# Start addresses of the large SBUF tiles in a two-block transformer kernel: from residue 128 to residue 0 modulo 2048 bytes

## The chip, the cores and the metric

The kernel runs on one NeuronCore of a Trainium2 chip. The metric is the device time of one execution in microseconds; the median of three runs before is 3795.62 us (3795.41 to 3798.67).

## The reference

The input is x, [1, 512, 1024] in float32: 512 tokens (T), width 1024 (D). Two blocks are computed.

- First block: an adaptive norm from a condition vector, one projection to eight times the width, a gated recurrence in eight heads, a gated depthwise convolution of 31 taps with a layer norm, a merge and an output projection; then an expert layer in which each token picks 16 of 16384 experts in each of eight heads. The kernel computes the expert layer as two dense products with a matrix of gates between them.
- Second block: a dilated-window attention with a squared-ReLU MLP of width 4096, then a differential attention with such an MLP, with norms ahead of each, and a last norm.

In outline:

```python
h = x + g1 * (merge(recurrence(u @ w_in), conv(u @ w_in)) @ w_out)
h = h + g2 * ((gelu(u2 @ U.T) * gates) @ V)          # 16384 experts, dense
for mix in (dilated_attention, differential_attention):
    h = h + mix(norm(h) @ w_qkv) @ w_o
    h = h + relu(norm(h) @ w_in) ** 2 @ w_out
```

All of it is in float32; nearly all of the arithmetic is in matrix products with 512 tokens as the moving side.

## The kernel before, in words

**Layout.** Activations stand transposed: partition p of tile [P, KT, T] holds feature 128 k + p of all 512 tokens. KT is 8, so such a tile has 8 slices of 512 float32 (2048 bytes) in each partition. The residual stays in `hT`.

**Panels.** Every large product is cut into panels: 128 output features by 1024 input features, 8 slices of 128x128 weights. There are 568 panels, kept in one list in the order of use (`panels`); the queue of SyncE loads them one after the other into a ring of four buffers (`ring`, `load`, L318 to L321). The first 16 are used by VectorE; the other 552 are *split* panels for TensorE.

**The split.** To keep the accuracy of float32 with one-pass float32r matmuls, a weight panel and its moving tile are each held as a high and a low part. ScalarE copies `ring` to `high_w` (rounded, L819 and L1096), GpSimd writes ring - high_w back into `ring_r` (L2014). `uT_r`, `ring_r` and `sq_r` are float32r names for the same bytes as `uT`, `ring` and `sq`. TensorE does three matmuls for each slice k (`panel`, L364 to L383), 24 for a panel, each with 512 moving columns and weights of its own:

```python
t_.matmul(out, wh, xh, start=(k == 0), stop=False)            # L377
t_.matmul(out, wh, xl, start=False, stop=False)               # L378
last = t_.matmul(out, wl, xh, start=False, stop=(k == KT-1))  # L379
```

wh is a slice of `high_w`, wl one of `ring_r`, and (xh, xl) is the moving pair. `two_panels` (L394 to L396) does the same for two panels at once. The pairs are:

| Panels | Count | xh, xl |
|---|---|---|
| heads and gates of the first block | 64 | uT_r, ulo (which is part_x) |
| w_a | 8 | sq_r, og_r (part0) |
| w_b | 8 | cvh (part_x), cv_r (part1) |
| w_out | 8 | uT_r, sga_r (part2) |
| peer_wq, expert up, qkv (twice), MLP up (twice) | 256 | uT_r, sq_r |
| expert down | 128 | part0, part1 or part2, part3 in turn |
| output projection of the attentions | 16 | kT_r (part1), qT_r (part0) |
| MLP down (twice) | 64 | part0, part1 or part2, part3 in turn |

So 208 panels stream both parts from `part0` to `part3`, 24 stream one of the two from there, and 320 neither.

**Order.** The order of the work is written out by hand for each engine in a function of its own; semaphores `w_slot`, `hi_ready`, `lo_ready`, `gemm_done` and `bank_free` hand a panel from SyncE's queue to ScalarE, GpSimd and TensorE and its result from PSUM to VectorE or ScalarE. VectorE makes the low and high parts of the hidden tiles (L1391, L1392) and adds each output panel to `hT` (L1716, L1719).

**Places in SBUF.** Tiles are placed one after the other, in the order in which they are declared, each at the next multiple of 32 bytes; the first of this program begins at byte 16,512 of each partition (8 x 2048 + 128). `arena` is 27520 float32, on which most other tiles are views; `part0` to `part3`, `between` and `part_x` are float32r names for stretches of it. This gives:

| Tile | First byte before | modulo 2048 |
|---|---|---|
| hT | 16512 | 128 |
| uT, uT_r | 32896 | 128 |
| ring, ring_r | 49280 | 128 |
| high_w | 65664 | 128 |
| sq, sq_r | 82048 | 128 |
| st | 98432 | 128 |
| cc, cst, ones, act_out | 106624, 108320, 109344, 109856 | 128, 1824, 800, 1312 |
| arena, part0 | 112640 | 0 |
| part1, part2, part3 | 129024, 145408, 161792 | 0 |
| part_x | 192640 | 128 |

A slice of weights takes 512 bytes in each partition, so slice k of a weight buffer begins at 128 + 512 k modulo 2048; a slice of a moving tile takes 2048 bytes.

Of the kernel before, what the change touches and what calls it, by code (L numbers as in the profile page):

```python
# [27 lines left out]
P = 128  # L28
T = 512
D = 1024  # L30
KT = D // P
# [33 lines left out]
NCOLS = _n  # L65
# [52 lines left out]
def build(nc, panels, xT, cols, consts, lmask, keysT, oh, rel, blam, ada_rest, outT, gdram, adram, btab, strips_dram):  # L118
    F32 = mybir.dt.float32
# [5 lines left out]
    with ctx:  # L125
        def sb(name, shape, dt=F32):
            return ctx.enter_context(nc.sbuf_tensor(name, shape, dt))

        F32R = mybir.dt.float32r
# [8 lines left out]
            return ctx.enter_context(nc.semaphore(name))  # L138

        ps = ctx.enter_context(nc.psum_tensor("ps", [P, 8, 512], F32))  # L140
        hT = sb("hT", [P, KT, T])
        BF16 = mybir.dt.bfloat16
        uT, uT_r = both("uT", [P, KT, T])
# [2 lines left out]
        sq, sq_r = both("sq", [P, KT, T])  # L146
        st = sb("st", [P, 4, T])
        ms, sr, rt, rstd = (st[:, n, :] for n in range(4))
        cc = sb("cc", [P, NCOLS])
        cst = sb("cst", [P, 2 * P])  # L150
        ones = sb("ones", [P, P])
        act_out = sb("act_out", [P, 1, T])
        rbs = sb("rbs", [35, 16])
        ada = sb("ada", [P, 48])
        small = sb("small", [P, 96])
        sb("to_128_bytes", [P, 24])
        with nc.sbuf_tensor("arena", [P, 27520], F32) as arena:
            pass

        parts = [sb(f"part{n}", [P, KT, T], F32R) for n in range(4)]  # L160
        between_r = sb("between", [P, 20000 - 4 * KT * T], F32R)
        part_x = sb("part_x", [P, KT, T], F32R)
        sb("rest", [P, 27520 - 20000 - KT * T])
        ident, iota = cst[:, 0:P], cst[:, P:2 * P]

        def view(at, *shape):
# [2056 lines left out]
```

How the kernel before makes its waits and increments, by code:

```python
    def wait(self):  # L90
        self.eng.wait_ge(self.sem, self.value())
# [6 lines left out]
    def wait_but_last(self):  # L99
        v = self.count - 1
        for reg, per in self.regs:
            v = reg * per + v
        self.eng.wait_ge(self.sem, v)
# [209 lines left out]
        @block.sync  # L314
# [3 lines left out]
            def load(i, j):  # L318
                sp.wait_ge(gemm_done, i * RING + (j + 1))
                sp.dma_start(ring[:, j], panels[i * RING + (RING + j)]).then_inc(w_slot[j], 16)
# [3 lines left out]
                sp.dma_start(gi[:, g, k, :].rearrange("p (a t) -> p a t", a=TT),  # L325
                             gdram[:, 8 * g + k:8 * g + k + 1].rearrange("a i j t -> j (i a) t")).then_inc(g_in[g], 16)
            at_gates = (8 * Q_PEER + 4 * PER_TILE * TT + 8) // RING
            with sp.Fori(0, at_gates) as i:
                for j in range(RING):
                    load(i, j)
            for j in range(RING):
                load(at_gates, j)
                if j == 0:
                    sp.wait_ge(g_out, 272)
                for k in range(4):
                    first_gates(j // 2, 4 * (j % 2) + k)
            with sp.Fori(0, 8 * Q_END // RING - 2 - at_gates) as i:
                for j in range(RING):
                    load(i + (at_gates + 1), j)
            for n in range(4):
                sp.wait_ge(u_ready, 50 + 2 * n)
                sp.dma_start(outT[:, 2 * n:2 * n + 2], sq[:, 2 * n:2 * n + 2]).then_inc(out_done, 16)
            sp.wait_ge(out_done, 64)
```

## Time and profile before

| | |
|---|---|
| Median of three runs | 3795.62 us |
| Span of the profiled execution | 3793.6 us |
| TensorE busy | 3674.0 us (97%), 16460 matmul records |
| VectorE busy | 2314.3 us (61%) |
| GpSimd busy | 1476.4 us (39%) |
| ScalarE busy | 1316.0 us (35%) |
| DMA | 486.59 MB, mean 128 GB/s |

The profile gives no time for its own execution beyond the span; the median of the runs is 2.0 us above that span, which is what lies around it. A matmul's duration in these rows (some 390 ns) overlaps with its neighbours', so what a matmul costs in a dense stretch is the distance from its start to the start of the next, its *pace*; a count of matmuls in a window holds the one or two that were already running when the window began.

### The profile page before, as it was taken

The page shows a single profiled execution, that of the slowest core. Times are in us where ns is not written, and L with a number is a line of the kernel's source. Part 1 is how long each engine was busy: PE and PEld are TensorE (multiplying, and loading weights), DVE is VectorE, ACT ScalarE, POOL GpSimd, SP SyncE. Part 2 cuts the span into 40 slices and gives each one's busy share as a digit, 9 for nine tenths or more (in the row PEclk, how much of TensorE's full clock was granted, in tenths as well). Part 3 has the DMA queues.
Part 4 walks back from the last instruction along what each step waited for, and adds up shares of the span by engine and source line. Part 5 has one row for each costly group of instructions (what it writes and reads, how often), then busy time and mean ns, then how long its engine had stood idle before and what let it go on. Part 6 is the DMA issues. An engine that isn't in the chain of part 4 may idle for free.

```text
span 3793.6 us, 48518 instructions
## 1 busy us (share of the span) xinstructions
PE 3674.0 (97%) x16460; PEld 2908.2 (77%) x16460; DVE 2314.3 (61%) x3639; ACT 1316.0 (35%) x1805; POOL 1476.4 (39%) x684
## 2 busy tenths in 40 slices
PE   6999999999999999999999999989999999999998
PEld 4787777788888888878888887855788877358886
DVE  5787996155757585188888775346564431658541
ACT  4554323334343434321111113246322232663221
POOL 2322443333333333344444443454344444124442
PEclk8999999999999999999999999989999999999999
DMA  5435322233546463865555652221222222112222
GB/s 203 150 109 189 113 89 79 90 98 120 188 146 193 137 214 116 261 215 186 186 185 184 197 174 90 95 68 44 67 95 99 96 89 99 59 46 92 95 98 79
DMA packets 267076, 486.59 MB, mean 128 GB/s; under 512 B 16770, under 2 KB 148226, under 8 KB 266658
## 3 DMA queue, kind: packets, MB, share of 16 engines
q1 hardware_dynamic: 90816, 304.12, 24.3%
q10 hardware_dynamic: 176132, 180.76, 14.6%
q8 instruction: 82, 1.34, 0.1%
q14 instruction: 46, 0.37, 0.0%
HBM read 415.48 MB, written 84.02 MB: 132 GB/s over the span
## 4 chain that ended last, share of the span: by engine, by line
PE 87%; DVE 5%; issue 4%; ACT 3%; DMA 1%; DVEq 0%; POOL 0%; SPq 0%; ACTq 0%; POOLq 0%
PE ps L377 25%; PE ps L378 25%; PE ps L379 25%; PE ps L617 3%; PE ps L716 2%; DVE ps L1665 1%; DMA ring<-panels 1%; PE ps L489 1%; PE ps L693 1%; PE ps L425 1%; PE ps L706 1%; PE ps L698 1%; ACT arena L1240 0%; PE ps L596 0%; ACT arena L1246 0%
## 5 line engine op out<-in xcount | busy, mean ns | idle before, releaser
L2014 POOL TENSOR_TENSOR ring_r<-ring,high_w 128x1024 fp32r<-128x1024 f32 x552 | 1361.0, 2467 | 2086.4 <-ACT high_w L819 1623.5
L377 PE MATMUL ps<-uT_r,high_w 128*128 128x512 f32 x2608 | 1037.9, 398 | 4.3 <-DVE part_x L1402 2.0
L379 PE MATMUL ps<-uT_r,ring_r 128*128 128x512 f32 x2608 | 1017.8, 390 | 0.0
L819 ACT ACTIVATE high_w<-ring 128x1024 fp32r<-128x1024 f32 x440 | 464.3, 1058 | 1272.2 <-PE ps L379 1112.4
L378 PE MATMUL ps<-sq_r,high_w 128*128 128x512 f32 x2032 | 791.2, 389 | 0.0
L378 PE MATMUL ps<-part,high_w 128*128 128x512 f32 x1840 | 728.5, 396 | 0.0
L377 PE MATMUL ps<-part,high_w 128*128 128x512 f32 x1664 | 670.3, 403 | 11.4 <-issue 4.9
L379 PE MATMUL ps<-part,ring_r 128*128 128x512 f32 x1664 | 658.8, 396 | 0.0
L377 PEld LDWEIGHTS ps<-uT_r,high_w 128*128 128x128 f32 x2608 | 491.7, 189 | 111.0 <-issue 12.0
L379 PEld LDWEIGHTS ps<-uT_r,ring_r 128*128 128x128 f32 x2608 | 490.8, 188 | 103.4
L1391 DVE SCALAR_TENSOR_TENSOR part<-arena 128x512 fp32r<-128x512 f32 x192 | 463.8, 2416 | 6.6
L378 PEld LDWEIGHTS ps<-sq_r,high_w 128*128 128x128 f32 x2032 | 381.8, 188 | 78.3 <-issue 1.9
L378 PEld LDWEIGHTS ps<-part,high_w 128*128 128x128 f32 x1840 | 348.1, 189 | 88.2 <-issue 8.2
L377 PEld LDWEIGHTS ps<-part,high_w 128*128 128x128 f32 x1664 | 314.5, 189 | 94.0 <-issue 13.7
L379 PEld LDWEIGHTS ps<-part,ring_r 128*128 128x128 f32 x1664 | 314.4, 189 | 74.5
L1719 DVE TENSOR_TENSOR hT<-ps,hT 128x512 f32<-128x512 f32 x80 | 55.4, 692 | 307.1 <-PE ps L379 307.0
L1716 DVE SCALAR_TENSOR_TENSOR hT<-ps,ada,hT 128x512 f32<-128x512 f32 x136 | 102.2, 751 | 185.5 <-PE ps L379 185.5
L1782 DVE TENSOR_TENSOR st<-cst,ps 128x512 f32<-128x512 f32 x128 | 87.6, 684 | 206.2 <-PE ps L617 181.7
L1093 ACT ACTIVATE act_out<-ps 128x512 f32<-128x512 f32 x112 | 67.0, 598 | 402.8 <-PE ps L379 346.1
L378 PE MATMUL ps<-part_x,high_w 128*128 128x512 f32 x512 | 201.5, 394 | 0.0
L1798 DVE TENSOR_TENSOR arena<-arena 128x512 f32<-128x512 f32 x192 | 140.3, 730 | 71.3 <-DMA arena<-gdram 68.6
L1392 DVE TENSOR_TENSOR part<-arena,part 128x512 fp32r<-128x512 f32 x192 | 145.4, 757 | 6.6
(323 smaller groups left out, 3815.7 us busy)
## 6 DMA issues: line engine op xcount, KB each, us to landing
ring<-panels SPq DMA_DIRECT2D x568, 512.0 KB, 3.4
gdram<-arena ACTq DMA_DIRECT2D x16, 2048.0 KB, 9.7
arena<-adram ACTq DMA_DIRECT2D x128, 256.0 KB, 2.7
adram<-act_out ACTq DMA_DIRECT2D x112, 256.0 KB, 3.8
arena<-gdram ACTq DMA_DIRECT2D x112, 256.0 KB, 5.0
arena<-ada_rest ACTq DMA_DIRECT2D x32, 512.0 KB, 4.1
strips_dram<-btab ACTq DMA_DIRECT2D x4, 3584.0 KB
arena<-strips_dram ACTq DMA_DIRECT2D x32, 448.0 KB, 3.2
```

The source lines that it names most:

```text
L377: t_.matmul(out, wh, xh, start=(k == 0), stop=False)
L378: t_.matmul(out, wh, xl, start=False, stop=False)
L379: last = t_.matmul(out, wl, xh, start=False, stop=(k == KT - 1))
L617: last = t_.matmul(ps[:, 6 + par, k * P:(k + 1) * P], brng[:, 4 * par + k, :], arng[:, 4 * par + k, :], start=True, stop=True)
L716: ins = t_.matmul(ps[:, 6 + (hh if s == 0 else 0), :], vs[:, par, kt, :], pt[:, hh if s == 0 else par, kt, :], start=(kt == 0), stop=(kt = ...
L819: s_.activation(high_w[:, j % RING], ring[:, j % RING], ACT.Copy).then_inc(hi_ready, 1)
L1391: S.done(v_.scalar_tensor_tensor(out=high, in0=src, scalar=1.0, in1=src, op0=ALU.mult, op1=ALU.max))
L1392: return v_.tensor_tensor(low, src, high, ALU.subtract)
L1716: ins = v_.scalar_tensor_tensor(out=hT[:, j, :], in0=ps[:, j % BANKS, :], scalar=ada[:, gain + j:gain + j + 1], in1=hT[:, j, :], op0=ALU.m ...
L1782: S.mark(v_.tensor_tensor(arng[:, four, :], keys, of_slots(0), ALU.is_equal))
L1798: S.done(v_.tensor_tensor(gel[:, j % 4, :], gel[:, j % 4, :], other, ALU.mult))
L2014: g_.tensor_tensor(ring_r[:, j], ring[:, j], high_w[:, j], ALU.subtract).then_inc(lo_ready, 1)
```

## The change

Only the placement of tiles changes. `cc` and `ada` are declared first, with a filler of 32 bytes, so that `hT` begins at 18432 (9 x 2048); `uT`, `ring`, `high_w`, `sq`, `st` and `arena` follow with no gap, each a multiple of 2048 long. `between` is 32 float32 shorter, so that `part_x` begins at 19968 float32 of the arena and not at 20000. `cst`, `ones`, `act_out`, `rbs` and `small` come behind the arena.

```diff
+        cc = sb("cc", [P, NCOLS])
+        ada = sb("ada", [P, 48])
+        sb("to_2048_bytes", [P, 8])
         hT = sb("hT", [P, KT, T])
...
-        cc = sb("cc", [P, NCOLS])
+        with nc.sbuf_tensor("arena", [P, 27520], F32) as arena:
+            pass
+
+        parts = [sb(f"part{n}", [P, KT, T], F32R) for n in range(4)]
+        between_r = sb("between", [P, 19968 - 4 * KT * T], F32R)
+        part_x = sb("part_x", [P, KT, T], F32R)
+        sb("rest", [P, 27520 - 19968 - KT * T])
         cst = sb("cst", [P, 2 * P])
         ones = sb("ones", [P, P])
         act_out = sb("act_out", [P, 1, T])
         rbs = sb("rbs", [35, 16])
-        ada = sb("ada", [P, 48])
         small = sb("small", [P, 96])
-        sb("to_128_bytes", [P, 24])
-        with nc.sbuf_tensor("arena", [P, 27520], F32) as arena:
-            pass
-
-        parts = [sb(f"part{n}", [P, KT, T], F32R) for n in range(4)]
-        between_r = sb("between", [P, 20000 - 4 * KT * T], F32R)
-        part_x = sb("part_x", [P, KT, T], F32R)
-        sb("rest", [P, 27520 - 20000 - KT * T])
```

Afterwards hT, uT, ring, high_w, sq, st, arena, part0 to part3 and part_x all have residue 0 modulo 2048 (weight slices 512 k), and cst, ones and act_out have 1536, 512 and 1024. No instruction is added, removed or moved.

## Rows read from the trace of the kernel before

**Rows 1.** The page: busy time by engine; TensorE's granted clock in 40 slices.
```profile
PE 3674.0 (97%) x16460; PEld 2908.2 (77%) x16460; DVE 2314.3 (61%) x3639; ACT 1316.0 (35%) x1805; POOL 1476.4 (39%) x684
...
PEclk8999999999999999999999999989999999999999
```

**Rows 2.** The page: the chain that ended last, shares of the span.
```profile
PE 87%; DVE 5%; issue 4%; ACT 3%; DMA 1%; DVEq 0%; POOL 0%; SPq 0%; ACTq 0%; POOLq 0%
PE ps L377 25%; PE ps L378 25%; PE ps L379 25%; PE ps L617 3%; PE ps L716 2%; DVE ps L1665 1%; DMA ring<-panels 1%; PE ps L489 1%; PE ps L693 1%; PE ps L425 1%; PE ps L706 1%; PE ps L698 1%; ACT arena L1240 0%; PE ps L596 0%; ACT arena L1246 0%
```

**Rows 3.** Windows: busy PE, PEld, DVE, ACT, POOL (count); clock, DMA share, GB/s.
```profile
725.00:800.00 75.00, 75.00 (x332) 61.80 (x330) 0.00 (x0) 21.41 (x28) 35.74 (x15) 1.00 0.31 103
...
3100.00:3175.00 75.00, 75.00 (x332) 62.11 (x331) 9.19 (x14) 14.38 (x14) 33.49 (x14) 1.00 0.30 99
...
1700.00:1775.00 75.00, 75.00 (x324) 60.80 (x324) 63.00 (x54) 13.80 (x13) 34.30 (x14) 1.00 0.53 176
...
1700.00:2300.00 600.00, 600.00 (x2583) 486.47 (x2583) 489.62 (x431) 113.62 (x107) 265.64 (x108) 1.00 0.55 183
...
2905.00:2925.00 20.00, 20.00 (x88) 16.08 (x87) 2.08 (x3) 3.19 (x4) 9.59 (x4) 1.00 0.31 105
```

**Rows 4.** Groups by line and shape: the matmuls of the split panels.
```profile
L377 PE MATMUL ps<-uT_r,high_w 128*128 128x512 f32 x2608 | 1037.9, 398 | 4.3 <-DVE part_x L1402 2.0 <-ACT arena L1087 1.0 <-ACT arena L1023 0.7
L378 PE MATMUL ps<-sq_r,high_w 128*128 128x512 f32 x2032 | 791.2, 389 | 0.0
L378 PE MATMUL ps<-part,high_w 128*128 128x512 f32 x1840 | 728.5, 396 | 0.0
L377 PE MATMUL ps<-part,high_w 128*128 128x512 f32 x1664 | 670.3, 403 | 11.4 <-issue 4.9 <-DVE part L1970 3.5 <-POOL ring_r L2014 2.2
L378 PE MATMUL ps<-part_x,high_w 128*128 128x512 f32 x512 | 201.5, 394 | 0.0
```

**Rows 5.** TensorE's timeline, MLP up panels: first and last start of 33 paces.
```profile
3459.87 0.39 PE L377 MATMUL ps<-uT_r,high_w 128*128 128x512 f32 x1
...
3467.35 0.39 PE L377 MATMUL ps<-uT_r,high_w 128*128 128x512 f32 x1
```

**Rows 6.** TensorE's timeline, expert down panels: first and last start of 28 paces.
```profile
1900.13 0.39 PE L377 MATMUL ps<-part,high_w 128*128 128x512 f32 x1
...
1906.63 0.39 PE L378 MATMUL ps<-part,high_w 128*128 128x512 f32 x1
```

**Rows 7.** TensorE's timeline, MLP down panels, first and last of 30 paces.
```profile
2910.05 0.39 PE L377 MATMUL ps<-part,high_w 128*128 128x512 f32 x1
...
2917.05 0.39 PE L377 MATMUL ps<-part,high_w 128*128 128x512 f32 x1
```

**Rows 8.** TensorE's timeline, w_b panels: first and last start of 27 paces.
```profile
634.51 0.40 PE L377 MATMUL ps<-part_x,high_w 128*128 128x512 f32 x1
...
640.81 0.40 PE L377 MATMUL ps<-part_x,high_w 128*128 128x512 f32 x1
```

**Rows 9.** TensorE's timeline behind a pause, at the lower clock: five paces.
```profile
3385.26 0.63 PE L378 MATMUL ps<-part,high_w 128*128 128x512 f32 x1
...
3387.39 0.63 PE L377 MATMUL ps<-part,high_w 128*128 128x512 f32 x1
```

**Rows 10.** Groups by line and shape: VectorE, GpSimd and ScalarE on tiles of either residue.
```profile
L1719 DVE TENSOR_TENSOR hT<-ps,hT 128x512 f32<-128x512 f32 x80 | 55.4, 692 | 307.1 <-PE ps L379 307.0
L1851 DVE TENSOR_TENSOR arena<-ps,st 128x512 f32<-128x512 f32 x16 | 11.1, 692 | 81.8 <-PE ps L379 81.8
L2092 POOL TENSOR_TENSOR part<-act_out,part 128x512 fp32r<-128x512 f32 x8 | 10.2, 1273 | 54.0 <-ACT part L1280 54.0
L2105 POOL TENSOR_TENSOR part<-arena,sq_r 128x512 fp32r<-128x512 f32 x8 | 10.4, 1294 | 9.5 <-ACT sq_r L1030 9.5
```

**Rows 11.** The page: the panel loads, KB each and us to landing.
```profile
ring<-panels SPq DMA_DIRECT2D x568, 512.0 KB, 3.4
```

## The prediction

> **What bounds the kernel now.** I read the busy shares first: TensorE is busy for 97% of the span at nearly full clock, the next engine for 61% [rows 1]. The chain that ended last agrees: 87% of it is TensorE, and the three matmul lines of the split panels alone are 75% [rows 2]. So the time is the number of those matmuls times their pace, plus stretches that have nothing to do with addresses. The change adds and removes no instruction; it can act only through what an instruction costs at another address. Since TensorE has no slack, the thing to read is the pace of the split matmuls, and whether it already differs between tiles of residue 128 and of residue 0.
>
> It does. Two windows of 75 us in which only uT_r and sq_r stream hold 332 matmuls each; the same length in the expert down panels, where only part0 to part3 stream, holds 324 [rows 3]. The timelines give it exactly: with uT_r and sq_r, 33 paces take 3467.35 - 3459.87 = 7.48 us, 226.7 ns each [rows 5]; in the expert down panels 28 paces take 6.50 us, 232.1 ns each [rows 6]; in the MLP down panels 30 paces take 7.00 us, 233.3 ns each [rows 7]. The mean durations show the same step: 389 ns for sq_r, 396 ns for part on the same line, L378 [rows 4]. In all of them the weights begin at 128 + 512 k; what differs is that uT_r, sq_r and part_x have the weights' residue (mod 512) and part0 to part3 do not.
>
> **Is it the address, and not the neighbours?** Against other engines as the cause: the pace is 226.7 in a window with no VectorE work and in one with 9.19 us of it, and 233.3 ns where VectorE works 2.08 of 20 us [rows 3, 7]. Against DMA: its share is 0.30 to 0.31 in both the fast windows and that slow one. Against a high address: part_x is the highest tile of all (192640), and with uT_r it is fast, as its mean of 394 ns in early panels, short stalls included, already suggests [rows 4]. Against the clock: it is granted at 1.00, 2.4 GHz, in all these windows [rows 3]. One mismatched stream in three is enough: in w_b, where only L378 streams from a part, 27 paces take 6.30 us, 233.3 ns [rows 8]. I read it as the stream of moving columns meeting the load of the next weights, which runs beside it: a matmul of 512 columns needs 213.3 ns at 2.4 GHz, the matched pace adds 13.4, the mismatched one 19 to 20. At the lower clock, five paces with mismatched tiles take 2.13 us, 426 ns each, which is 512 columns at 1.2 GHz and nothing more [rows 9]; so the extra is time in which something with a limit of its own cannot feed the faster array.
>
> **The change part by part.**
>
> 1. *part0 to part3 come to the residue of the weights* (by moving the weights to 0). If only the relation counts, their panels go to the matched pace, 226.7 ns.
>    - Expert down: 128 panels x 24 = 3072 matmuls. The window of 600 us holds 2583, less about two that straddle its edge, 232.5 ns each [rows 3]. Gain 5.8 ns x 3072 = 17.8 us.
>    - MLP down and attention output: 80 panels x 24 = 1920 matmuls at 233.3 [rows 7]; some of them run at the 232.1 of rows 6, so I take 6.3 ns: 12.1 us.
>    - w_a, w_b, w_out: 24 panels x 24 = 576 at 233.3 [rows 8]: 3.8 us. Ahead of w_b TensorE waits for the layer norm, so some of it is lost in that wait; I take 2.5 us.
>    - Sum 32.4 us, on TensorE, which is the chain here. What is late next in the down panels: VectorE is busy 489.62 of 600 us, 82% [rows 3], and at a period 2.5% shorter 84%; GpSimd goes from 44 to 45%. Neither becomes the bound.
> 2. *uT_r, sq_r, part_x and the weights all go from 128 to 0 together.* Their relation stays, so I price the 320 panels at nothing. Nothing hides it if that is wrong: each ns of pace is 7680 x 1 ns = 7.7 us. No long warm stretch of rows has both sides at residue 0, so this is the unknown. Its bounds from rows: up to the mismatched 232.1 to 233.3 on one side (+41 to +51 us), down to the bare 213.3, which half of the 426 ns at the lower clock gives [rows 9], on the other (-103 us). I take zero, because a pattern of 128 against 128 and one of 0 against 0 differ in nothing that the rows show to matter.
> 3. *hT, st, cst, ones, act_out change places.* VectorE takes 692 ns to add PSUM to hT, where every SBUF operand has residue 128, and 692 ns for a product read from st (128) and written to the arena at residue 1024; GpSimd takes 1273 ns with act_out (1312) and 1294 ns with arena and sq_r (0 and 128) [rows 10]. Nothing to gain; between those rows, 0 to 2% of engines with slack.
> 4. *The ring's rows land at 512-byte boundaries.* A panel lands in 3.4 us [rows 11] and DMA is 1% of the chain, about 40 us, in the first 100 us and in the heads [rows 2]. I take 0; from 1 us worse to 2.5 better. The Trainium skill (DMA: Bandwidth & Descriptors, How a descriptor splits into AXI transactions) says that a descriptor which does not start at a multiple of 256 bytes costs one more transaction. For rows of 4096 bytes that would be 17 in place of 16; applied to those 40 us it makes an estimate of 2.4 us less, and no row here shows it.
>
> The sum is -32.4 us. The profiled span is 3793.6 and the median of the runs 2.0 above it; 3795.6 - 32.4 = 3763. Own range of this case: 3758 (MLP and output panels all at 6.6 ns, nothing lost in waits, DMA 2.5 us better, 37 in all) to 3770 (a fifth of the gain lost in new waits).
>
> **The rivals.**
>
> *Nothing changes (3796).* The slow pace belongs to part0 to part3 for a reason that the residue does not touch, for instance that they are the middle of the address range (112640 to 178176) or are the tiles of the hidden stages. For it: no run here moves a tile, all four slow tiles are neighbours, and one mismatched stream in three costs as much as three. Against it: the pace steps with the operand's name within one stage, and part_x, beyond them, is fast. The Trainium skill (TensorE: Matmul & The Clock Gate, Step-by-step: what each phase is for) says that weights and moving columns have independent read ports, so that loading the next weights takes no bandwidth from the running matmul. By that rule no residue could matter and the time would stay at 3796. The trace does not bear it out as it stands: two paces for the same instruction, 226.7 and 232 to 233 [rows 5, 6].
>
> *Slower (3842).* What costs is a moving stream that begins at residue 0, whatever the weights have. Then part0 to part3 stay slow and the fast tiles join them: 7680 matmuls x 5.4 to 6.6 ns = +41 to +51 us, 3837 to 3846. It decides as soon as the window that holds 332 matmuls in the up panels holds 324. For it: the rows fit it just as well, since a moving tile of residue 0 is always the slow one. Against it: a tile of residue 0 touches one block of 2048 bytes and one of residue 128 two, so it is hard to see why the first should lose. The one thing that makes it possible is that the relation was never varied alone.
>
> *Much faster (near 3600).* Full alignment takes away the 13.4 ns of the matched pace as well: 552 x 24 = 13248 matmuls x 13.4 = 177 us on top of 32. For it: the overhead is absent at the lower clock [rows 9]. Against it: a matched pair already shows the 13.4 in every long stretch.
>
> **How the numbers follow.** A measurement of this kernel can tell about 0.2%, 7.6 us, from no change. The matched case has 0.62, nothing 0.18, slower 0.16, much faster 0.04. The range leaves out the last two, 0.20 together, and takes in the matched case and no change with its scatter: 3757 to 3800. The forecast's own range is 3758 to 3770. Chance of faster 0.66, within 0.2% 0.18, slower 0.16.
>
> **What would show it.** Right: windows of 75 us in the expert down panels hold 332 matmuls, as in the up panels; the mean durations on L378 are one number for sq_r and part; the span of the up panels is unchanged; all of the gain lies from 550 to 700, 1630 to 2360 and in the down and output panels behind. Wrong: the down panels still hold 324 (no change), or the up panels fall to 324 (slower). A gain outside the down panels would be one that I have not priced.

## The result and the profile after

The changed kernel takes 3764.37 us (median of four runs, 3763.71 to 3766.29) against 3795.51 us for the kernel before (median of four, one more than the three above); the ratio is 0.9921, 95% interval 0.9908 to 0.9934. The profiled span is 3761.9 us, 31.7 us less than before. The forecast was 3763.

The page of the kernel after, busy times, clock and chain, beside [rows 1, 2]:

```profile
span 3761.9 us, 48518 instructions
...
PE 3643.5 (97%) x16460; PEld 2903.7 (77%) x16460; DVE 2314.3 (62%) x3639; ACT 1315.9 (35%) x1805; POOL 1477.6 (39%) x684
...
PEclk8999999999999999999999999989999999999999
...
PE 86%; DVE 5%; issue 4%; ACT 3%; DMA 1%; DVEq 0%; POOL 0%; SPq 0%; ACTq 0%; POOLq 0%
```

The instructions and their counts are the same. TensorE is busy for 30.5 us less, VectorE, ScalarE and GpSimd for the same time within 1.2 us. So nothing was done elsewhere; the same matmuls take less.

Windows of the kernel after, with the columns of [rows 3]:

```profile
3075.00:3150.00 75.00, 75.00 (x332) 62.12 (x331) 8.99 (x13) 14.14 (x14) 33.52 (x14) 1.00 0.30 99
...
1700.00:1775.00 75.00, 75.00 (x332) 61.80 (x331) 64.60 (x57) 14.01 (x14) 32.21 (x13) 1.00 0.56 185
1700.00:2300.00 600.00, 600.00 (x2642) 494.71 (x2641) 492.59 (x435) 116.90 (x110) 272.82 (x110) 1.00 0.55 184
```

Before, 75 us of the expert down panels held 324 matmuls and 75 us of the up panels 332; now both hold 332, and the 600 us hold 2642 in place of 2583. The groups by line and shape, beside [rows 4]:

```profile
L377 PE MATMUL ps<-uT_r,high_w 128*128 128x512 f32 x2608 | 1037.6, 398 | 4.6 <-DVE part_x L1402 2.0 <-ACT arena L1087 1.0 <-ACT arena L1023 0.7
L378 PE MATMUL ps<-sq_r,high_w 128*128 128x512 f32 x2032 | 791.0, 389 | 0.0
L378 PE MATMUL ps<-part,high_w 128*128 128x512 f32 x1840 | 718.6, 391 | 0.0
L377 PE MATMUL ps<-part,high_w 128*128 128x512 f32 x1664 | 662.0, 398 | 11.6 <-issue 4.9 <-DVE part L1970 3.6 <-POOL ring_r L2014 2.2
```

On L378 the mean of a part went from 396 to 391 ns and that of sq_r stayed at 389; on L377 part went from 403 to the 398 that uT_r has, before and after. The timeline of TensorE in the expert down panels, 30 paces in 6.80 us, 226.7 ns each, where [rows 6] had 232.1:

```profile
1899.93 0.39 PE L377 MATMUL ps<-part,high_w 128*128 128x512 f32 x1
...
1906.73 0.39 PE L377 MATMUL ps<-part,high_w 128*128 128x512 f32 x1
```

**Where the 31.7 us lie.** The first matmul of the expert down panels and the first one behind them, in the timeline of the kernel before:

```profile
1634.60 0.77 PE L377 MATMUL ps<-part,high_w 128*128 128x512 f32 x1 [4.89 <-issue]
...
2361.09 0.79 PE L377 MATMUL ps<-uT_r,high_w 128*128 128x512 f32 x1
```

and in that of the kernel after:

```profile
1632.97 0.76 PE L377 MATMUL ps<-part,high_w 128*128 128x512 f32 x1 [4.90 <-issue]
...
2343.32 0.79 PE L377 MATMUL ps<-uT_r,high_w 128*128 128x512 f32 x1
```

| Stretch | Before | After | Gain | Priced |
|---|---|---|---|---|
| start to the expert down panels | 1634.6 | 1633.0 | 1.6 | 2.5 |
| expert down panels | 726.5 | 710.4 | 16.1 | 17.8 |
| both attentions, both MLPs, end | 1432.5 | 1418.6 | 13.9 | 12.1 |
| span | 3793.6 | 3761.9 | 31.7 | 32.4 |

The last of these stretches has a part in it that was not priced. Its first attention runs, without any split panel, from the first row of each pair to just before the second. In the kernel before:

```profile
2498.45 0.60 PE L673 MATMUL ps<-cst,arena 128*128 128x128 f32 x4
...
2667.08 0.47 PE L377 MATMUL ps<-part,high_w 128*128 128x512 f32 x1 [2.26 <-DVE part L1970]
```

and in the kernel after:

```profile
2480.68 0.60 PE L673 MATMUL ps<-cst,arena 128*128 128x128 f32 x4
...
2647.47 0.47 PE L377 MATMUL ps<-part,high_w 128*128 128x512 f32 x1 [2.26 <-DVE part L1970]
```

That is 168.6 us before and 166.8 after. The second attention took 145.9 and 145.0. Together they gave 2.7 of the 13.9 us.

### The profile page after: what moved, and what is told of

Its sections match the earlier page's. It is cut to its first block, busy times and chain, and to the rows that moved or that the text cites. A ratio compares the mean times of both kernels' runs of the same rounds, so it can differ in the third digit from the quotient of the medians.

```text
span 3761.9 us, 48518 instructions
## 1 busy us (share of the span) xinstructions
PE 3643.5 (97%) x16460; PEld 2903.7 (77%) x16460; DVE 2314.3 (62%) x3639; ACT 1315.9 (35%) x1805; POOL 1477.6 (39%) x684
## 4 chain that ended last, share of the span: by engine, by line
PE 86%; DVE 5%; issue 4%; ACT 3%; DMA 1%; DVEq 0%; POOL 0%; SPq 0%; ACTq 0%; POOLq 0%
PE ps L377 25%; PE ps L378 25%; PE ps L379 25%; PE ps L617 3%; DVE ps L1665 2%; PE ps L716 2%; DMA ring<-panels 1%; PE ps L489 1%; PE ps L693 1%; PE ps L425 1%; PE ps L706 1%; ACT arena L1240 1%; PE ps L698 1%; PE ps L596 0%; PE ps L420 0%
## 5 line engine op out<-in xcount | busy, mean ns | idle before, releaser
L377 PE MATMUL ps<-uT_r,high_w 128*128 128x512 f32 x2608 | 1037.6, 398 | 4.6 <-DVE part_x L1402 2.0
L378 PE MATMUL ps<-sq_r,high_w 128*128 128x512 f32 x2032 | 791.0, 389 | 0.0
L378 PE MATMUL ps<-part,high_w 128*128 128x512 f32 x1840 | 718.6, 391 | 0.0
L377 PE MATMUL ps<-part,high_w 128*128 128x512 f32 x1664 | 662.0, 398 | 11.6 <-issue 4.9
L379 PE MATMUL ps<-part,ring_r 128*128 128x512 f32 x1664 | 649.8, 391 | 0.0
L377 PEld LDWEIGHTS ps<-uT_r,high_w 128*128 128x128 f32 x2608 | 491.5, 188 | 111.5 <-issue 12.3
L378 PEld LDWEIGHTS ps<-sq_r,high_w 128*128 128x128 f32 x2032 | 381.8, 188 | 78.4 <-issue 1.9
L1391 DVE SCALAR_TENSOR_TENSOR part<-arena 128x512 fp32r<-128x512 f32 x192 | 435.0, 2265 | 6.6
L378 PEld LDWEIGHTS ps<-part,high_w 128*128 128x128 f32 x1840 | 347.1, 189 | 79.0 <-issue 8.4
L377 PEld LDWEIGHTS ps<-part,high_w 128*128 128x128 f32 x1664 | 313.5, 188 | 88.4 <-issue 16.1
L378 PE MATMUL ps<-part_x,high_w 128*128 128x512 f32 x512 | 201.8, 394 | 0.0
L1392 DVE TENSOR_TENSOR part<-arena,part 128x512 fp32r<-128x512 f32 x192 | 172.4, 898 | 6.6
```

Source lines behind the costliest of these rows:

```text
L379: last = t_.matmul(out, wl, xh, start=False, stop=(k == KT - 1))
L1391: S.done(v_.scalar_tensor_tensor(out=high, in0=src, scalar=1.0, in1=src, op0=ALU.mult, op1=ALU.max))
L1392: return v_.tensor_tensor(low, src, high, ALU.subtract)
```

## The experiments

The time alone does not say which property of the new addresses counts. Three theories fit it. **A**: the relation between the start of the moving tile and the start of the weights. **B**: the weights must lie on 512-byte boundaries. **C**: the tiles must begin at multiples of 2048. In the kernels below only placement is changed, by fillers or by another order of declaration; no instruction is added, removed or moved.

### Everything at 128, and the weights apart from the rest

all_128 puts every tile of the argument at residue 128:

```diff
-        sb("to_2048_bytes", [P, 8])
+        sb("to_2048_bytes", [P, 40])
```

> The changed kernel with a filler of 160 bytes in place of 32, so that hT, uT, ring, high_w, sq, st, the arena, part0 to part3 and part_x all begin at residue 128 modulo 2048. Theory A (only the relation of the moving tile's start to the start of the weights counts): every split matmul at the matched pace of 226.7 ns, 332 matmuls in 75 us of the expert down panels, 3764 us. Rival B (weights must lie on 512-byte boundaries for part0 to part3 to be fast) and rival C (the tiles must begin at multiples of 2048): the part panels stay at 232 to 233 ns, 324 in 75 us, 3790 to 3800 us.

Measured: 3764.93 us (median of four), ratio to the kernel before 0.9924 (0.9907 to 0.9941), span 3763.6. The timeline in the expert down panels has 21 paces in 4.76 us, 226.7 ns each:

```profile
1900.03 0.39 PE L377 MATMUL ps<-part,high_w 128*128 128x512 f32 x1
...
1904.79 0.39 PE L377 MATMUL ps<-part,high_w 128*128 128x512 f32 x1
```

B and C fall: neither 512-byte boundaries nor multiples of 2048 are needed.

weights_0_rest_128 leaves the weights at 0 and moves all else:

```diff
         sb("to_2048_bytes", [P, 8])
+        ring, ring_r = both("ring", [P, RING, KT, P])
+        high_w = sb("high_w", [P, RING, KT, P], F32R)
+        sb("shift", [P, 32])
         hT = sb("hT", [P, KT, T])
...
-        ring, ring_r = both("ring", [P, RING, KT, P])
-        high_w = sb("high_w", [P, RING, KT, P], F32R)
```

> The two weight buffers begin at residue 0, every moving tile and the arena at 128. Theory A: every split panel is mismatched, all 13248 matmuls at 232 to 233.3 ns, so 13248 x 5.4 to 6.6 = 72 to 87 us more than the changed kernel, less what waits hide: 3830 to 3850 us. Rival B: the weights lie on 512-byte boundaries, so everything is fast, 3764 us. Rival C (a moving tile off a multiple of 2048 crosses a block and pays): slow too, but then all_128 is slow as well.

Measured: 3829.82 us (median of four), ratio 1.0101 (1.0084 to 1.0118), span 3827.3. Now uT_r is slow too; the timeline in panels with uT_r and sq_r (lines one further down than before) has 60 paces in 14.00 us, 233.3 ns each, where the kernel before had 226.7 [rows 5]:

```profile
749.83 0.39 PE L380 MATMUL ps<-uT_r,ring_r 128*128 128x512 f32 x1
...
763.83 0.39 PE L380 MATMUL ps<-uT_r,ring_r 128*128 128x512 f32 x1
```

weights_128_rest_0 is the mirror image: hT, uT, sq, st and the arena at 0, then a filler of 128 bytes ahead of the weights:

```diff
+        sb("shift", [P, 32])
         ring, ring_r = both("ring", [P, RING, KT, P])
         high_w = sb("high_w", [P, RING, KT, P], F32R)
+        cst = sb("cst", [P, 2 * P])
+        ones = sb("ones", [P, P])
+        small = sb("small", [P, 96])
```

> The mirror image: every moving tile and the arena begin at residue 0, the two weight buffers at 128. Theory A: all 13248 matmuls at 232 to 233.3 ns, 3830 to 3850 us, the same as with weights at 0 and the rest at 128. Rival B: slow, 3830 to 3850 us. Rival C: 3764 us, since the moving tiles are at multiples of 2048.

Measured: 3825.6 us, span 3823.8; 61 paces in 14.18 us, 232.5 ns, in the same stage:

```profile
749.80 0.39 PE L378 MATMUL ps<-uT_r,high_w 128*128 128x512 f32 x1
...
763.98 0.39 PE L379 MATMUL ps<-sq_r,high_w 128*128 128x512 f32 x1
```

So both residues are fast together and slow apart, whichever side has which. These two were expected at 3830 to 3850 us and came in at the lower edge and 4 us below it. The paces are the expected ones, but the 13248 x 5.8 = 77 us of longer matmuls show as 65 and 62 us of span. TensorE is busy for 71.5 and 66.2 us more than in the changed kernel (3715.0 and 3709.7 against 3643.5), and its idle time falls from 118.4 us to 112.3 and 114.1: some of the longer work lies in time in which TensorE waited before. Which waits shrank I have not itemised.

### What distance counts

For these, one filler ahead of the arena shifts part0 to part3 and part_x against weights, uT and sq at 0 (here 256 bytes; the others have 8, 16, 24, 48, 56 and 128 float32):

```diff
+        sb("shift", [P, 64])
         with nc.sbuf_tensor("arena", [P, 27520], F32) as arena:
```

> The changed kernel with the arena (part0 to part3 and part_x) moved up by 512 bytes; uT, sq and the weights stay at 0. Slices of weights begin at multiples of 512 anyway and the pace of before did not change with the slice. Theory A with a period of 512 bytes or less: 226.7 ns everywhere, 3764 us. If the relation counts modulo 2048: the 208 part panels at 232 to 233, and those 72 with part_x and uT or sq slower too, 280 to 296 panels x 24 x 5.4 to 6.6 ns = 36 to 47 us more, about 3805 us.

> The changed kernel with the arena (part0 to part3, part_x) moved up by 256 bytes, the rest at 0: 280 panels have one or both moving streams at residue 256 to the weights' 0 (modulo 512). Theory A1 (any offset modulo 512 that is not 0 costs the same): those panels at 232 to 233 ns, 280 x 24 x 5.7 = 38 us, less what waits hide, 3795 to 3805 us. Theory A2 (the period is 256 bytes or less, as 0 and 128 alone would also fit): 226.7 ns everywhere, 3764 us.

> The same with 32 bytes, the smallest step in which tiles are placed. A1: as with 256, 3795 to 3805 us. A2 with a period of 128 or 256 bytes: also slow, since 32 is no multiple. Theory A3 (what counts is whether moving columns and weights lie in the same line of 128 bytes or more at the same time, and 32 bytes shift only a quarter of them): between, 3770 to 3785 us.

> The changed kernel with the arena moved up by 64 bytes. A1: 3795 to 3805 us, the same pace of 232 to 233 ns in the part panels as with 32, 128 and 256. A2 with a period of 64 bytes would make this one fast (3764 us), but then 128 had been fast too, which it was not. A3: the shift is half of a line, so between arena_32 and the 232 to 233 ns of 128.

> The same with 96 bytes. Offsets of 32, 64 and 128 gave 233.3, 231.1 and 232.7 ns in the part panels. If only multiples of 256 are matched: 231 to 233.5 ns, 3787 to 3803 us.

> The changed kernel with the arena moved up by 192 bytes, that is 64 below the next multiple of 256. If the distance to the nearest multiple of 256 counts, whichever side, the part panels are at the 231.1 ns of 64 bytes, 3787 us. If the order of the two streams counts, another pace; below 226.7 ns would be a placement better than the changed kernel's (under 3760 us), which I hold for unlikely.

> The same with 224 bytes, 32 below the next multiple of 256. By distance alone: the 233.3 ns of 32 bytes in the part panels, about 3800 us. By order: another pace, and if the moving stream just behind the weights is what collides, 226.7 ns and 3764 us.

A shift of the arena touches 296 panels (208 + 24 + the 64 that stream part_x), not the 280 of these expectations; at 5.7 ns that makes 40 us in place of 38.

Each is one run, and the kernel before measured 3788 to 3805 us beside them on its runs, so the times are good to some 10 us; the paces are the firmer reading. The counts are of 75 us of the expert down panels (1800 to 1875) and of 25 us of MLP down panels (2825 to 2850).

| Shift, bytes | Time, us | Span, us | Matmuls in 75 us | in 25 us |
|---|---|---|---|---|
| 0 (the changed kernel) | 3764.4 | 3761.9 | 331 | 112 |
| 32 | 3803.6 | 3801.8 | 323 | 109 |
| 64 | 3787.0 | 3785.2 | 323 | 111 |
| 96 | 3800.8 | 3799.0 | 323 | 109 |
| 192 | 3796.7 | 3794.9 | 323 | 109 |
| 224 | 3798.9 | 3797.1 | 323 | 109 |
| 256 | 3766.1 | 3764.3 | 331 | 112 |
| 512 | 3762.2 | 3760.4 | 332 | 112 |

The windows of four of them (shifts of 256, 224, 64 and 32 bytes), one fence for each kernel:

```profile
1800.00:1875.00 75.00, 75.00 (x331) 61.78 (x330) 62.62 (x57) 14.88 (x14) 33.79 (x14) 1.00 0.60 198
```
```profile
1800.00:1875.00 75.00, 75.00 (x323) 60.38 (x322) 62.03 (x55) 13.53 (x13) 31.77 (x13) 1.00 0.59 187
```
```profile
1800.00:1875.00 75.00, 75.00 (x323) 60.77 (x322) 59.87 (x55) 14.52 (x14) 31.99 (x13) 1.00 0.60 191
```
```profile
1800.00:1875.00 75.00, 75.00 (x323) 60.22 (x323) 62.04 (x55) 13.84 (x13) 31.82 (x13) 1.00 0.56 180
```

A shift of 256 or 512 bytes costs nothing; every one of 32, 64, 96, 192 and 224 does, and 128 does by the two kernels above. So theory A stands with a period of 256 bytes (A2), and neither A1's period of 512 nor a price that grows with the distance (A3) does. The kernels also hold their own control. With the shift of 32 bytes, uT_r and sq_r, which were not moved, keep the matched pace; 63 paces take 14.28 us, 226.7 ns each:

```profile
749.68 0.39 PE L380 MATMUL ps<-uT_r,ring_r 128*128 128x512 f32 x1
...
763.96 0.39 PE L380 MATMUL ps<-uT_r,ring_r 128*128 128x512 f32 x1
```

In all of these the weights lie at 0, and the only common residue other than 0 that any kernel here has is 128. That both sides at, say, 32 or 64 are fast too would follow from the rule but was not run. No offset gave a pace under the matched 226.7 ns, so none of these beats the changed kernel; 3762.2 us for the shift of 512 is within its scatter.

Two expectations of this series missed. By A1 and A2 the shift of 64 was to cost 31 us or more, and it cost 23; its two stages differ. The timeline of the shift of 64, expert down (31 paces in 7.23 us, 233.2 ns) and MLP down (44 paces in 10.07 us, 228.9 ns):

```profile
1804.62 0.40 PE L378 MATMUL ps<-part,high_w 128*128 128x512 f32 x1
...
1811.85 0.40 PE L379 MATMUL ps<-part,high_w 128*128 128x512 f32 x1
...
2819.82 0.39 PE L378 MATMUL ps<-part,high_w 128*128 128x512 f32 x1
...
2829.89 0.39 PE L380 MATMUL ps<-part,ring_r 128*128 128x512 f32 x1
```

The same instructions on the same tiles run at two paces. The kernel before had this too, 232.1 and 233.3 ns [rows 6, 7]. A mismatched stream has more than one steady pattern, and what decides which one it takes, for instance what ran ahead of it or what the other engines do meanwhile, I did not test. The 231.1 ns that later expectations give for 64 bytes lies midway between its two paces; no timeline of that kernel has it. The shift of 192, expected to mirror 64 at 3787 us, took 3796.7 and is at 109 in 25 us where 64 is at 111.

### One of the three weight loads off

ring_128 and high_w_128 keep all moving tiles at 0 and place one weight buffer at 128 (shown for ring; high_w the same way):

```diff
         st = sb("st", [P, 4, T])
+        sb("shift", [P, 32])
+        ring, ring_r = both("ring", [P, RING, KT, P])
+        cst = sb("cst", [P, 2 * P])
+        ones = sb("ones", [P, P])
+        small = sb("small", [P, 96])
```

> All moving tiles, the arena and high_w at residue 0, ring alone at 128: of the three weight loads of a slice one (L379) is at another residue than the streams. Theory A with the pattern of the w_b panels before (one mismatched stream in three costs as much as three): all 552 panels at about 233 ns, 3825 to 3832 us, as with both weight buffers off. If the cost is per mismatched load: a third of it, 2 ns a matmul, 3783 to 3790 us.

> All moving tiles, the arena and ring at residue 0, high_w alone at 128: of the three weight loads of a slice two (L377, L378) are off. ring alone off measured 231.1 ns, 4.3 ns over the matched pace. If every mismatched load had its own price, this one would be at 226.7 + 2 x 4.3, 235 ns, above the 232.7 of both off; if the stalls delay each other as in w_b before, it is at 232 to 233 ns, 552 panels, about 3820 to 3830 us.

Measured: 3805.9 us (span 3804.2) with ring off and 3834.2 us (span 3832.4) with high_w off. The timelines in panels with uT_r and sq_r: ring off, 61 paces in 14.10 us, 231.1 ns:

```profile
749.69 0.39 PE L378 MATMUL ps<-uT_r,high_w 128*128 128x512 f32 x1
...
763.79 0.40 PE L379 MATMUL ps<-sq_r,high_w 128*128 128x512 f32 x1
```

high_w off, 60 paces in 14.00 us, 233.3 ns:

```profile
749.82 0.40 PE L380 MATMUL ps<-uT_r,ring_r 128*128 128x512 f32 x1
...
763.82 0.40 PE L380 MATMUL ps<-uT_r,ring_r 128*128 128x512 f32 x1
```

One load in three off costs 4.4 ns a matmul, two in three 6.6, three in three 5.8 to 6.6. Ring off met neither of its two expectations (a third of the price, or all of it). high_w off was expected at 3820 to 3830 us and came in 4 us above. The price is not a sum over mismatched loads: one load off already costs two thirds to three quarters of what three cost, and one stream in three off, in w_b, cost all of it [rows 8]. Two of three off is no better than all three (3832.4 against 3823.8 and 3827.3 us of span).

## Why the prediction was right

**The bound.** The pace of the split matmuls sets the time. All the gain is TensorE's (busy 30.5 us less, span 31.7), and no other engine became the bound: VectorE is busy 492.59 of the 600 us of down panels, 82%, where 84% was priced.

**Step 1, parts at the residue of the weights.** Right. The pace went from 232.1 to 233.3 to the matched 226.7 ns. The sizes are each off a little: 16.1 us for the expert down panels where 17.8 were priced, since the price set the mean of a 600 us window, which has the restarts between panels in it, against a pace without restarts; the like pair is 2642 against 2583 matmuls in 600 us, 5.2 ns each, 16.0 us. The MLP and attention stretches gave 13.9 for 12.1, but the 80 panels that were priced there gave only 11.1 of it. An MLP down stage of eight panels took 44.8 us before and 43.5 after, 6.7 ns for each of 192 matmuls where I had taken 6.3. The last two stages of each MLP, directly one behind the other, gave less, 2.3 us together, so that all 64 MLP panels gave 9.7 us, 6.3 ns a matmul. The 16 output panels gave 1.5 us, 3.9 ns a matmul. The other 2.7 us lie in the two attentions, where no split panel runs. The prediction had priced nothing there, and no run shows it to be an effect of the change: the first attention takes 166.8 us in the changed kernel, 169.2 in all_128, as matched as it, and 166.1 in arena_96, which is mismatched.

The first block gave 1.6 for 2.5. Its part with w_a, w_b and w_out went from 414.4 us (386.5 to 800.9) to 411.7 (387.6 to 799.3), 2.7 us less, and all that lies ahead of it took 1.1 us more. But with the shift of 256, which is matched as well, that part takes 414.1 us, so this term is not shown within its own size. The forecast is closer than its terms: they erred both ways, and that 32.4 met 31.7 is in part luck. What is firm is the expert down and MLP down panels, 25.8 of the 31.7 us.

**Step 2, all of it going from 128 to 0 priced at nothing.** This was the unknown, and right: uT_r and sq_r keep 398 and 389 ns, and their windows 332 matmuls. all_128 shows why, which before was argued and not shown: 128 with 128 and 0 with 0 are the same thing. Its time is the changed kernel's, 3764.93 against 3764.37.

**Steps 3 and 4.** VectorE's addition to hT is at 691 ns (692 before). A panel still lands in 3.4 us. The first split matmul starts at 48.81 us, before at 48.89: the transfers ahead of it gained nothing that shows. The Trainium skill (DMA: Bandwidth & Descriptors, How a descriptor splits into AXI transactions) has an extra transaction for rows off a 256-byte boundary; by the prediction's estimate that would have been 2.4 us. It is not borne out here, as far as landing times given to 0.1 us tell: as an estimate, one transaction in 17 is 0.2 us of a landing of 3.4.

**The rivals.** *Nothing changes* fell with the result. The Trainium skill (TensorE: Matmul & The Clock Gate, Step-by-step: what each phase is for) has the next weights load through a port of their own, at no cost to the running matmul; that does not hold here as stated. With the moving tiles at residue 0 throughout, the residue of the weight buffers decides between 226.7 ns (the changed kernel) and 232.5 or 233.3 (weights_128_rest_0, high_w_128). Whether it is the ports at which the two meet, no run shows. *Slower, since a start at 0 is what costs* fell with the result and with weights_0_rest_128, in which no moving tile begins at 0 and all are slow. *Much faster* fell too: the 13.4 ns above 213.3 stay in every placement tried, at the full clock.

What the prediction could not see was the period. I wrote the relation as one of residues modulo 512; it is modulo 256. The change's own 2048 is eight times what is needed.

## What to carry to other kernels

Where float32r matmuls of 512 columns stream back to back with new weights for each, start the moving tiles and the weight buffers at the same residue modulo 256 bytes (0 and 128 are the ones tried). Here that was worth 2 to 3% of the time such a stretch takes, and it costs a filler of under 256 bytes and an order of declaration. Look for it by comparing the number of matmuls in equal windows of two stages with the same shape: a stage that holds 324 where another holds 332, with TensorE busy throughout and the clock at full, has no wait that explains it, and where its operands lie is the next thing to look at. One operand off among several cost from two thirds of the price to all of it, so check every tile and buffer in the stream, low and high parts both.

## What the runs showed of the hardware that was not expected

- The matched pace of a 512-column float32r matmul with its own weight load is 226.7 ns at 2.4 GHz, 13.4 over the 213.3 of its columns, at residues 0 and 128 alike. At 1.2 GHz the same stream, mismatched, had 426 ns, the bare columns [rows 9]. A matched one has that too: in the kernel before, early in the first block, at a granted clock of 0.50, eight paces of uT_r and part_x take 3.41 us, 426 ns each. So neither the 13.4 ns nor the price of a mismatch shows at the lower clock.

```profile
49.45 0.63 PE L378 MATMUL ps<-part_x,high_w 128*128 128x512 f32 x1
...
52.86 0.55 PE L377 MATMUL ps<-uT_r,high_w 128*128 128x512 f32 x1
```

- Offsets between moving tile and weights of 32, 64, 96, 128, 192 and 224 bytes cost 5 to 7 ns a matmul in the expert down panels; 0, 256 and 512 cost nothing.
- A mismatched stream has several steady paces: 228.9 and 233.2 ns at the same offset of 64 bytes, 232.1 and 233.3 at 128. The matched stream had 226.7 wherever it was read without a stall.
- One weight load in three off costs 4.4 of the 5.8 to 6.6 ns that three cost. What in the reading of the two operands makes them collide, and why with a period of 256 bytes, stays open; these runs measured only its price.
